# A hybrid encoder layer on one core: half of a weight sum and the last gate tables, moved to GpSimd as larger pieces

## The reference, cut to what matters

```python
logits = (hf @ w_router + b_router)
topv, topi = lax.top_k(logits, 4)
gates = jax.nn.softmax(topv, axis=-1)
# assignments sorted by expert, padded to blocks of 128 rows of one expert
def expert_block(e, tok, gt):
    xb = hf[tok]
    g = minimum(xb @ w_gate[e] + b_gate[e], 7)
    u = clip(xb @ w_up[e] + b_up[e], -7, 7)
    act = (u + 1) * (g * sigmoid(1.702 * g))
    return (act @ w_down[e] + b_down[e]) * gt[:, None]
```

## Time and profile before

| what | value |
|---|---|
| median of three runs | 2149.92 us |
| the profiled execution's own time | 2147.94 us |
| its span (first to last record) | 2146.1 us |
| TensorE busy in the span | 97% |
| VectorE busy | 57% |
| ScalarE busy | 30% |
| GpSimd busy | 27% |
| mean granted TensorE clock | 0.985 of full |
| items in the loop, split items among them | 48, 23 |

### The profile page before, as it was taken

One profiled execution on the slowest core, in us unless ns is written; L12 is line 12 of the kernel. 1 busy time (PEld: TensorE's weight loads), 2 busy tenths in 40 slices (PEclk: granted clock), 3 DMA queues, 4 the chain that ended last, 5 costly groups with the idle time before them and its releaser, 6 DMA issues.

```text
span 2146.1 us, 35452 instructions
## 1 busy us (share of the span) xinstructions
PE 2071.0 (97%) x11374; PEld 902.7 (42%) x11375; DVE 1230.0 (57%) x2403; ACT 646.1 (30%) x1252; POOL 578.8 (27%) x537
## 2 busy tenths in 40 slices
PE   8999999995999999999998999999998999999997
PEld 6547677453333343333333333333333333344343
DVE  4322898586675465467363636626643676566753
ACT  2000888122232332222223223322223122232332
POOL 3181124224222222122132222221213122132323
PEclk9999999996999999999999999999999999999998
DMA  8000200128658777678969786685989868677775
GB/s 302 21 37 17 104 1 1 65 103 322 245 189 315 266 260 263 249 255 301 326 219 355 263 299 237 238 292 194 319 308 372 317 236 292 242 259 258 254 258 190
DMA packets 151911, 485.21 MB, mean 226 GB/s; under 512 B 20288, under 2 KB 37973, under 8 KB 151310
## 3 DMA queue, kind: packets, MB, share of 16 engines
q1 hardware_dynamic: 116192, 444.81, 54.8%
q0 software_dynamic: 33792, 34.66, 8.3%
q10 hardware_dynamic: 1874, 5.02, 0.6%
HBM read 461.26 MB, written 43.09 MB: 235 GB/s over the span
## 4 chain that ended last, share of the span: by engine, by line
PE 91%; DMA 4%; SPq 2%; DVE 1%; issue 1%; DVEq 0%; POOL 0%; ACT 0%; ACTq 0%; POOLq 0%
PE psum L2278 25%; PE psum L2307 15%; PE psum L2047 14%; PE psum L1719 7%; PE psum L2093 5%; PE psum L1825 4%; PE psum L1858 3%; DMA weights<-in_w_down 3%; PE psum L1818 3%; PE psum L1715 2%; PE psum L2004 2%; PE psum L2034 2%; PE psum L2105 1%; PE psum L2302 1%; PE psum L1867 1%; DMA weights<-in_w_up 1%
## 5 line engine op out<-in xcount | busy, mean ns | idle before, releaser
L775 POOL DMA_INDIRECT residual_rows<-work x184 | 340.8, 1852 | 538.6 <-ACT work L996 488.5
L2278 PE MATMUL psum<-x,work 128*64 128x512 f32 x1472 | 330.2, 596 | 1.9 <-DVE work L1555 1.6
L2307 PE MATMUL psum<-weights,work 128*128 128x512 f32 x736 | 325.4, 595 | 0.0
L2047 PE MATMUL psum<-weights,work 128*64 128x512 f32 (+2 forms) x1536 | 299.1, 595 | 0.6
L1548 DVE TENSOR_TENSOR x<-weights 128x2048 f32<-128x2048 f32 x92 | 206.7, 2288 | 108.4 <-PE psum L2285 64.2
L2278 PE MATMUL psum<-weights,work 128*64 128x512 f32 x1104 | 254.1, 603 | 7.0 <-DMA weights<-in_w_up 4.1
L732 POOL DMA_INDIRECT work<-normed_rows,work x47 | 52.4, 1116 | 645.5 <-PE psum L2004 493.1
L1548 DVE TENSOR_TENSOR x<-weights,x 128x2048 f32<-128x2048 f32 x92 | 208.2, 2283 | 6.1 <-DMA weights<-in_w_up 6.1
L2307 PEld LDWEIGHTS psum<-weights,work 128*128 128x128 f32 x736 | 136.1, 190 | 155.3 <-issue 154.0
L1405 DVE SCALAR_TENSOR_TENSOR work<-psum,work 128x4 f32<-128x4 f32 x47 | 7.4, 157 | 310.3 <-PE psum L1999 310.3
L2278 PEld LDWEIGHTS psum<-x,work 128*64 128x64 f32 x1472 | 101.3, 137 | 194.8 <-issue 190.0
(11 more groups left out here) (303 smaller groups left out, 2626.7 us busy)
## 6 DMA issues: line engine op xcount, KB each, us to landing
weights<-in_w_gate SPq DMA_DIRECT2D x64, 2048.0 KB, 7.9
weights<-in_w_up SPq DMA_DIRECT2D x64, 2048.0 KB, 12.5
weights<-in_w_down SPq DMA_DIRECT2D x64, 2048.0 KB
residual_rows<-x SPq DMA_DIRECT2D x9, 512.0 KB, 2.9
normed_rows<-work ACTq DMA_DIRECT2D x9, 512.0 KB, 2.7
x<-in_x SPq DMA_DIRECT2D x8, 512.0 KB, 8.8
weights<-in_w_in SPq DMA_DIRECT2D x16, 256.0 KB, 9.3
weights<-in_w_in SPq DMA_DIRECT2D x8, 512.0 KB, 12.3
```

The lines of the kernel that those rows point to most:

```text
L775: pl.indirect_dma_start(acc_d[:, :], bass.IndirectOffsetOnAxis(dest[:, b:b + 1], 0), yrow[:, b * BLK:(b + 1) * BLK], None, bounds_check=UN ...
L2047: mm = pe.matmul(out.rearrange("p (m n) -> p m n", m=2), xT[:, k, lo:lo + cols], wgu[:, :, k, blk * BLK:(blk + 1) * BLK], start=(k == 0), ...
L2278: mm = pe.matmul(out, tokens[:, k, :], weights[:, :, k, g * BLK:(g + 1) * BLK], start=start and k == 0, stop=ends and k == 3)
L2307: mm = pe.matmul(bank(4 + h), actT[:, k, :], wdn[:, k, h * HALF:(h + 1) * HALF], start=False, stop=(k == DT - 1))
```

## The change

Four edits:

1. `weight_sum(3, 1)` leaves VectorE. GpSimd's loop gets, ahead of the gather, a branch on the item's token code. For a split item it reads two more values (the item's expert, and the number of split items before it) from the tables, waits for `s_prod` at 3n+3, computes the same half sum (128 x 2048), and counts `s_parts` up by 2.
2. VectorE now makes seven counted weight sums for one split item, so all waits on `s_wts` go from 8n to 7n. SyncE's load of k-blocks 4 to 7 waits for `s_parts` too. TensorE's last sum product waits for both halves ahead of its first k-step; before, it waited for each half ahead of that half's k-steps.
3. The gate tables of token tiles 4 to 7 are made in one pass: the same eight steps on 4 times as many elements, in place in `pick`, after all gates are there.
4. VectorE copies the parts of the second item's expert (`own_parts`) ahead of that item's row numbers, not behind them.

```diff
@@ SyncE
-                sp.wait_ge(s_wts, 8 * n + (WTS0 - 2))
+                sp.wait_ge(s_wts, 7 * n + (WTS0 - 1))
                 for m in range(2):
                     load_gu(m, 0, bass.ds(e, 1))
-                sp.wait_ge(s_wts, 8 * n + WTS0)
+                sp.wait_ge(s_wts, 7 * n + WTS0)
+                sp.wait_ge(s_parts, 2 * n + TT)
                 sp.wait_ge(s_gu, UNIT * last + (UNIT - 1))
@@ GpSimd
+            def last_gate_parts(lo):
+                pl.wait_ge(s_gates, TT)
+                block = pick[:, lo:, :, :]
+                link(pl.tensor_tensor(block, block, gate[:, lo:, :].unsqueeze(3).to_broadcast([P, TT - lo, TOP_K, EXPERTS]),
+                                      ALU.mult))
+                for n in (2, 1):
+                    link(pl.tensor_tensor(block[:, :, 0:n, :], block[:, :, 0:n, :], block[:, :, n:2 * n, :], ALU.add))
+                rest = block[:, :, 0, :]
+                for c in (3, 4):
+                    link(pl.tensor_copy(parts_i[:, lo:, :, c], rest))
+                    link(pl.tensor_tensor(rest, rest, parts_i[:, lo:, :, c], ALU.subtract))
+                pl.tensor_copy(parts_i[:, lo:, :, 5], rest).then_inc(s_parts, TT - lo)
...
-            for i in range(4, TT):
-                gate_parts(i)
-
+            last_gate_parts(4)
             gather_rows(1)
...
                 with pl.If(j < n_items - 1):
+                    code = pl.value_load(items[0:1, bass.ds(j + TABLE, 1)], min_val=1, max_val=SPLIT + SEQ)
+                    with pl.If(code > SPLIT):
+                        own = pl.value_load(items[0:1, bass.ds(j, 1)], min_val=0, max_val=EXPERTS - 1)
+                        n = pl.value_load(splits[0:1, bass.ds(own, 1)], min_val=0, max_val=EXPERTS)
+                        pl.wait_ge(s_prod, 3 * n + 3)
+                        pl.tensor_tensor(sums[:, 1, :, 2:4, :], wgt_half(1, 1)[:, :, 2:4, :], sums[:, 1, :, 2:4, :],
+                                         ALU.subtract).then_inc(s_parts, 2)
                     gather_rows(j + 2)
@@ VectorE
             compare()
+            dve.wait_ge(s_parts, TT)
+            own_parts(bass.ds(e1, 1)).then_inc(s_own, 1)
             dve.wait_ge(s_ips0, 2)
             first_row_numbers(second_rows_out)
-            dve.wait_ge(s_parts, TT)
-            own_parts(bass.ds(e1, 1)).then_inc(s_own, 1)
...
-                dve.wait_ge(s_wts, 8 * n + (WTS0 + 2))
+                dve.wait_ge(s_wts, 7 * n + (WTS0 + 2))
...
-                dve.wait_ge(s_wts, 8 * n + (WTS0 + 4))
+                dve.wait_ge(s_wts, 7 * n + (WTS0 + 4))
...
                 dve.tensor_tensor(kept[:, 0], unit_bank(1), kept[:, 2], ALU.add).then_inc(s_u, 1)
-                weight_sum(3, 1)
                 gated(j, 0)
@@ TensorE
                 def summed(c, to, tokens, start, ends):
+                    if c == 3:
+                        pe.wait_ge(s_wts, 7 * n + (WTS0 + 7))
+                        pe.wait_ge(s_parts, 2 * n + (TT + 2))
                     for k in range(4):
-                        if k % 2 == 0:
-                            pe.wait_ge(s_wts, 8 * n + (WTS0 + 2 * c + k // 2 + 1))
+                        if k % 2 == 0 and c < 3:
+                            pe.wait_ge(s_wts, 7 * n + (WTS0 + 2 * c + k // 2 + 1))
                         mm = product(to, tokens, sums[:, c % 2], k, start, ends)
```

## The result

| | before | after |
|---|---|---|
| median | 2149.92 us | 2219.05 us |
| lowest and highest of 5 | 2148.78, 2150.6 | 2213.84, 2223.31 |
| profiled execution: time, span | 2147.94, 2146.1 | 2223.31, 2221.6 |

The ratio is 1.032, with a 95% interval of 1.0308 to 1.0332: slower by 69 us. The forecast was 2210 in a range of 2180 to 2236.

The account below looks back on a forecast made before the run. TensorE, busy 97% of the span, was taken to bound the kernel by its work plus gaps. Early 9, mid 13, late 30, clock 8, less 0.3 at the start, made 60 us on 2147.94: median 2210 us, range 2180 to 2236.

Parts of the forecast that it names:

- mid items: 11 split items, adds landed 1.7 to 2.0 us before T (VectorE's start on sum 1): 1.2 us each, 13 us.
- rows named as signs: Profile after: TensorE's and transposes' waits, GpSimd row of 4.5 (6 to 7 if held), longer VectorE rows, clock at 0.50.
- first rival: Mid items: GpSimd gets in ahead of half 0, 2.3 us each; +72 us in all, 2222 us; chance 0.25.
- late items: 7 split items, adds landed at T+3.9 to T+4.0: last sum product starts 4.3 us later each, 30 us.
- Who began first holds: SBUF exclusion: an operation of GpSimd or VectorE blocks the other's of these kinds for its whole length.
- early: 5 split items, adds landed 3.0 to 7.7 us before T: three lose 1.6, two 2.0; 9 us.
- late, clock: TensorE behind late items' gaps: lower clock may lose 1.75 us each; five taken, 8 us.
- start of the loop: Gate tables in one pass save 7 us, first item 2.5 earlier, but down weights limit the gain to 0.3 us.
- the place that the forecast named: At 534.77 TensorE waits 0.35 us for the second half of the down weights, a transfer that does not start earlier.
- second rival: Only VectorE's one-input fast operations are excluded; only late items and their clock cost: 38 us, 2188 us; chance 0.08.
- third rival: VectorE's chain is relieved: TensorE keeps at most 8.5 us, most likely 3; 2141 to 2147 us; chance 0.03.
- fourth rival: No change: GpSimd's sum in a misjudged shadow and a few late items absorbed; chance 0.03.

Follow-up runs that it names:

- the tables' own run: Kernel before with only edits 3 and 4 (gate tables of tiles 4 to 7 in one pass, own_parts moved): 2148.89 us, ratio 1.0002.
- with pieces: Changed kernel with GpSimd's half sum as four operations of 512 elements: 2205.12 us, ratio 1.0251 to the kernel before.
- the late-wait run: Changed kernel with TensorE waiting for GpSimd's half only before k-step 2 of the last sum product: 2205.81 us, ratio 1.0254 to the kernel before.

## Why the prediction was right, and where it was off

**Direction and mechanism: right, but for the mid items.** The chain of VectorE's work up to unit 2 sets TensorE's third transpose; the two engines exclude each other for whole operations; GpSimd is late in some items. Most of the rows named as signs are there: transposes that wait for VectorE, a GpSimd row of 4.5, a `kept[1]` of several us, waits of TensorE for GpSimd of about 4, falls of the clock behind them. Two are not: no GpSimd row of 6 to 7, and no wait of TensorE for GpSimd of 0.6 in the mid items, where it waits 0.5 for VectorE's half 0. In the mid items the first rival is what happened, and the 2219 us measured are nearer to its 2222 than to the 2210 of the forecast. That the late items' sum came out near is partly luck: one item fewer and a shorter gap took 7 us off, and the clock put 7 on.

**GpSimd's duration.** Forecast 4.5 from 512 and 1024 elements; measured 4.53. Right.

**When GpSimd is ready: the mis-sized term.** I put 3.4 us between the wait for the adds (L780) and the sum, most of it from one value load measured at 0.85. Measured, it is 2.85. That half microsecond decided the mid items: the forecast had GpSimd ready at T+1.4 to T+1.7, behind half 0's start at T+1.33, and a loss of 1.2; it was ready at T+0.8 to T+0.9, got in ahead of half 0 and cost 2.25. This is the first rival's mechanism, at the price that it gave (2.3), and I had it at 0.25. "Who began first holds" failed there: GpSimd had waited behind `kept[1]`, and half 0 came next in VectorE's order but did not get the port. The estimate's margin was smaller than its error.

**Counts.** Forecast 5 early, 11 mid, 7 late; found 8, 8, 6 and one done ahead. The classes come from how far the adds' landing lies from T, and each loss moves the next item. The shares differ between executions, too, so counts from the profile before were good only to a few items.

| term | forecast | measured |
|---|---|---|
| early | 5 items, 9 us | 8 items, 14.2 |
| mid | 11 x 1.2 = 13 | 8 x 2.25 = 18.0 |
| late, the gap | 7 x 4.3 = 30 | 6 x 3.9 = 23.4 |
| late, clock | 8 | 38.3 - 23.4 = 14.9 |
| item with its sum ahead of T | none | 1.4 |
| start of the loop | -0.3 | +1.3 |
| clock behind the first early item | 0 | 1.7 |
| elsewhere | 0 | 0.6 |
| all | 60 | 75.5 |

(The 75.5 is of the profiled executions; between the medians it is 69. 3.9 is GpSimd's end at T+11.4 less the T+7.51 of before.)

**Early items.** 1.6 forecast and 1.70 measured where GpSimd is ready at T: right. The 2.0 was forecast for the two items at T-3.0, which lost 1.70, since GpSimd was ready there too. In one item the adds landed at T-2.4; GpSimd started at T+0.45, and it lost 2.02, by the mechanism of the forecast. The first item lost 1.97 for another reason: GpSimd starts at T+0.12, and VectorE idles 0.48 us before unit 2's last step, where it idles 0.22 in another early item.

**Clock.** The forecast took 1.75 behind five of seven late items. It came behind all six and cost 2.5 each, since in five of them it lasted 6.83 us and not the 3.41 of the earlier trace rows. The shorter gaps in mid items cost no clock in this profile, as assumed. The last sum product shows the size directly: in the six late items it lasts 5.35 to 6.57 us, 6.2 in the mean, in place of 3.65.

**Gate tables.** The pass itself: forecast 6.5 us, measured 503.51 to 509.75, 6.2. But the first item began 1.4 us sooner, not 2.5, and of this 0.8 was there before the pass began: GpSimd issued the first gather at 502.26, against 503.02 in the profile before. In the kernel after, VectorE's timeline, GpSimd's and TensorE's:

```profile
502.66 1.95 DVE L1446 TENSOR_SCALAR work<-work 128x32 f32<-128x32 f32 x1
```

```profile
503.51 1.05 POOL L753 TENSOR_TENSOR work<-work 128x512 f32<-128x512 f32 x1
```

```profile
517.77 5.56 PE L2052 MATMUL psum<-weights,work 128*32 128x256 f32 x64 [0.57 <-issue]
...
526.33 0.65 PE L2022 MATMUL psum<-ident,work 128*128 128x128 f32 x4 [3.00 <-DMA work<-normed_rows,work]
...
535.88 1.93 PE L2135 MATMUL psum<-weights,work 128*32 128x256 f32 x32 [1.38 <-DMA weights<-in_w_down]
```

TensorE's timeline in the kernel before:

```profile
526.25 0.65 PE L2004 MATMUL psum<-ident,work 128*128 128x128 f32 x4 [1.40 <-DMA work<-normed_rows,work]
```

VectorE's operation is done when GpSimd's is, at 504.6, though it had begun 0.85 us ahead of it; why it did not end before is not shown. GpSimd's wider operations hold up VectorE's item table, whose chain is 2.3 us longer. I had applied the exclusion in the loop and forgotten it here. What was won was gone at 526.3, ahead of the place that the forecast named: TensorE waits there for the second item's gathered rows, 3.00 us in place of 1.40. The down weights then landed 1.1 us later than before (a wait of 1.38 for 0.35), so the start became 1.3 us slower. In the tables' own run this came to nothing measurable.

**The second rival** (only one-input operations are excluded) is refuted by `kept[1]` and by half 0, both with two SBUF inputs. The Trainium skill's page "Perfetto Trace Analysis", section "Optimizing Scalar/DVE Operations", names the lock for a "2-port DVE op" alone; the rows here show it for two-input `tensor_tensor` as well. Another page of the Trainium skill, "SBUF — State Buffer", section "Who interferes with whom", does state that a VectorE operation with two SBUF inputs contends with a GpSimd operation reading SBUF; this case's 0.69 that became 4.48 agrees.

**The third rival** (faster through relief, 3 us most likely and 8.5 at most) had the size of the relief right: without the half there are 6.5 us. But GpSimd's hold took more from the same chain in every item, so the change could not reach them; the fourth rival (no change) goes with it.

**What stays open.** Why the clock stays low for 3.4 us behind some gaps and 6.8 behind others was not tried, nor was what decides how many items are late in an execution. That the port goes to GpSimd when it waits while VectorE passes from one operation to the next is read from all mid items of a profile (eight here, nine when the changed kernel was run again); with pieces the turns alternate, which fits. Nothing was run to find the arbitration's rule.

## What to carry to other kernels

Before moving work from VectorE to GpSimd, count what VectorE will be able to do meanwhile: with SBUF-to-SBUF work of its own beside it, a GpSimd operation of twice the length cost VectorE more than it saved in every placement that was run. First leave the work out in an experiment, which shows the most that moving it can bring (here 6.5 us); then look for that gain by reordering the chain, as moving four tiny operations behind unit 2 did, since that costs nothing. When an estimated start decides who gets a shared port, treat the two outcomes as equally likely if its error reaches across the point.

## What the hardware showed that was not expected

- A waiting GpSimd operation got the port between two VectorE operations that stood back to back, in all eight mid items: its row lasts 4.87 to 5.03 (4.53 and the rest of `kept[1]`), half 0's 6.62 in place of 2.28.
- Four GpSimd operations of 512 elements shared the port better than one of 2048: a VectorE operation beside them waited 1.1 us for one piece, not 4.3 for the whole.
- GpSimd's sum of 2048 elements made a VectorE operation of 4 elements a partition last 3.77 us in place of 0.16. Being small did not shorten its wait.
- A gap of 3.9 us in otherwise full work cost TensorE 2.5 us more in clock. Behind gaps of 1.8 to 2.1 us in the same place, in the late-wait run's profile, it cost nothing.
